# State products of eight running sequences: two products of 64 rows with eight masked blocks, or two of 32 rows with four

## The chip, the cores and the metric

The kernel runs on one core of a Trainium2 chip. The metric is the device time of one execution in microseconds (us). Three executions of the kernel before took 2974.32, 2974.84 and 2976.30 us; the median is 2974.84.

## The reference

The program is one step of a decoder layer: a gated feed-forward block, a mixer, and a second feed-forward block. The mixer has an attention half and a half with a linear recurrence (HGRN2), merged by one output projection. Two request groups share the weights: a prompt of 256 tokens, and 8 running sequences (NB) that each bring 8 new tokens (TS) and a recurrent state. Only the recurrence of the running sequences is touched here. Per sequence b and head h it ends with

```
S = jnp.exp(b_last)[..., None] * S + jnp.einsum(
    'bhsd,bhse->bhde', kc * jnp.exp(b_last[:, :, None] - b), vc)
```

S is a 128 x 128 matrix, kc the decayed keys of the sequence's 8 tokens (8 x 128), vc their values (8 x 128). There are 8 heads and 8 sequences, so 64 such state updates. Everything is float32.

## The kernel before, in words

**Where the work stands.** The recurrence and the first part of the output projection are written out by hand in "beats" (BEATS = 20); each engine has its own loop over the same beats (mix_pe, mix_act, mix_dve), and SyncE issues the loads and stores in mix_sync. Beats 0 to 9 do the four prompt chunks and the scores of the running sequences; beats 10 to 17 do heads 0 to 7 of the running sequences (pe_head, dve_head); beats 12 to 19 the normalisation of each head's output (pe_head_sum, act_head_root, dve_head_scale). The table OUT_AT puts one tile of the output projection (pe_out, 24 products of 128 x 128 by 128 x 320 each, lines L1744 to L1746) into beats 0 to 10, 12, 14, 17, 18 and 19; the tiles 16 to 31 follow after the beats. So head 1 and head 2 stand side by side on TensorE, as do 3 and 4, and 5, 6 and 7, and there is a tile of the projection between the groups.

**One head on TensorE (pe_head).** First the head's outputs: one product of the masked scores with the values (L1902), then for each of the 8 sequences a product of its old state with the decayed queries, 8 columns each (L1904). Then the state products (L1913): the 64 new tokens of all 8 sequences lie on 64 partitions, kst holds the keys (64 x 128 for a head). The values have been copied 8 times into vm, copy b multiplied by a column of gsel that is one on the rows of sequence b and zero elsewhere. A product of kst (64 rows) with four such copies (64 x 512) gives the updates of four sequences in one PSUM bank. There are two: sequences 0 to 3 to bank 6, 4 to 7 to bank 7. A float32 product runs as two passes in the records, each with its own weight load, so the two products are four matrix instructions (32 for the eight heads).

**ScalarE (act_head_values, L1939)** makes the masked copies: 8 activations of 64 x 128 per head, with double buffering over heads. Those of heads 0 and 1 are in beat 9, behind a Silu over all output gates (L2014); those of head h are in beat h + 9.

**VectorE (dve_head)** copies the head's outputs out of PSUM (L1923), multiplies the old states of all 8 sequences by their decay (L1924, 128 x 1024), waits for the state products (semaphore h_sd) and adds bank 6 and bank 7 to the states (L1928, two of 128 x 512). In later beats it normalises the outputs (dve_head_scale: a reciprocal, L1963, and two products, L1966 and L1968), splits them into high and low parts (L1712), and does the evictions and splits of the projection (L1733, L1725).

**What waits for what.** The state products of head h wait for vm of head h (h_vm), and for the adds of head h - 1 (h_sn), which have to empty banks 6 and 7. The copies of head h + 2 wait for the products of head h. Tile 16 of the projection is the first that needs the normalised heads (x_lo), the last of which VectorE makes in beat 20. The old states of heads 4 to 7 are loaded into the buffers of heads 0 to 3 once those have been stored (state_out, state_in).

Of the kernel before, what the change touches and what calls it, by code (L numbers as in the profile page):

```python
# [20 lines left out]
P = 128  # L21
D = 2048
KT = D // P
TP, NB, TS = 256, 8, 8
# [62 lines left out]
def build(nc, io, scr):  # L87
    ctx = ExitStack()
    with ctx:
# [3 lines left out]
        def at(name, off, shape, dt=F32):  # L93
            n = 4
            for d in shape[1:]:
                n *= d
            assert off * KB + n <= 207.8 * KB, (name, off, n)
            return nc.alloc_sbuf_tensor_at(name, shape, dt, offset=BASE + -(-int(off * KB) // 32) * 32)

        s = Sems(lambda n: ctx.enter_context(nc.semaphore(n)))  # L100
        bank = [ctx.enter_context(nc.psum_tensor(f"bank{i}", [P, 512], F32)) for i in range(8)]
# [21 lines left out]
        table = at("table", 3.09375, [33, HEADS])  # L123
        ptab = at("ptab", 3.1875, [1, NB * NPG], I32)
        mask_s = at("mask_s", 3.5, [64, 64])
        gsel = at("gsel", 3.75, [64, NB])
        caus = at("caus", 3.8125, [64, 64])
        kcs = at("kcs", 4.125, [P, 2, NB * 64])
        vcs = at("vcs", 8.125, [64, NB, G * HD])
# [104 lines left out]
        ort = at("ort", 72.625, [P, T])  # L234
        vt = at("vt", 92.125, [P, 3, HG * P])
        kst = at("kst", 104.125, [P, HG * P])
        vm_ = at("vm", 140.125, [64, 2, NB, P])
        dq_ = at("dq", 180.125, [P, 2, HG, 64])
        qi_ = at("qi", 184.125, [P, 2, HG, 64])
        osq_h = at("osq_h", 188.125, [P, 2, T])  # L240
# [835 lines left out]
        def wait_state(eng, h):  # L1076
            eng.wait_ge(s[f"s0_ld{h % SLOTS}"], 16 * (h // SLOTS + 1))
# [812 lines left out]
        def head_bank(h):  # L1890
            return bank[(5, 2)[h % 2]][:, 0:NB * TS]

        def pe_head(pe, h):
            wait_state(pe, h)
            if h == 0:
                pe.wait_ge(s["h_o"], 4)
                pe.wait_ge(s["h_am"], 17)
                pe.wait_ge(s["h_kst"], 10)
            if h >= 2:
                pe.wait_ge(s["h_oe"], h - 1)  # L1900
            o = head_bank(h)
            pe.matmul(o, vt[0:64, 2, h * P:(h + 1) * P], am[0:64, h, :], start=True, stop=False, skip_group_check=True)  # L1902
            for b in range(NB):
                mm = pe.matmul(o[:, TS * b:TS * b + TS], s0[h % SLOTS][:, b, :], qi_[:, 0, h, TS * b:TS * b + TS],  # L1904
                               start=False, stop=b == NB - 1, skip_group_check=True)
            mm.then_inc(s["h_so"], 1)
            pe.wait_ge(s["h_vm"], h + 1)
            if h:
                pe.wait_ge(s["h_sn"], 2 * h)
            else:  # L1910
                pe.wait_ge(s["h_st"], 4)
            for k in range(2):
                mm = pe.matmul(bank[6 + k][:, :], kst[0:64, h * P:(h + 1) * P],  # L1913
                               vm_[:, h % 2, 4 * k:4 * k + 4, :].rearrange("p b e -> p (b e)"), start=True, stop=True)
            mm.then_inc(s["h_sd"], 1)

        def dve_head(dve, link, h):
# [13 lines left out]
        def act_head_values(act, h):  # L1931
            if h == 0:
                act.wait_ge(s["h_sub"], 5 * NC + 2)
                act.wait_ge(s["hv_evd"], 3)
                act.wait_ge(s["h_ebc"], NC + 1)
            if h >= 2:
                act.wait_ge(s["h_sd"], h - 1)
            for b in range(NB):
                ins = act.activation(vm_[:, h % 2, b, :], vt[0:64, 2, h * P:(h + 1) * P], ACT.Copy, scale=gsel[:, b:b + 1])  # L1939
            ins.then_inc(s["h_vm"], 1)  # L1940

# [29 lines left out]
        def mix_pe(pe):  # L1971
            pe_in(pe)
            pe.wait_ge(s["ev"], EV_IN)
            pe.wait_ge(s["s_o"], 4 * NB + 1)
            pe_att_sums(pe)
            pe.wait_ge(s["hv_eva"], 3)
            pe.wait_ge(s["hv_evd"], 3)
            for b in range(BEATS):
                if b < 2 * (NC + 1):
                    if b % 2 == 0:  # L1980
                        pe_hgrn_scores(pe, b // 2)
                    elif b // 2 < NC:
                        pe_hgrn_results(pe, b // 2)
                elif b - 10 < HG:
                    pe_head(pe, b - 10)
                if b >= 12:
                    pe_head_sum(pe, b - 12)
                if b in OUT_AT:
                    pe_out(pe, OUT_AT[b])
            for i in range(KT, N_OUT):  # L1990
                pe_out(pe, i)

        def mix_act(act):
# [9 lines left out]
            for b in range(BEATS + 1):  # L2003
                if b in OUT_AT:
                    act_out(act, OUT_AT[b] + 1)
                if b < 2 * (NC + 1):
                    if b % 2 == 0:
                        if b // 2 < NC:
                            act_decays(act, b // 2 + 1)
                        act_keys(act, b // 2)  # L2010
                    elif b // 2 < NC:
                        act_carried(act, b // 2 + 1)
                    else:
                        act.activation(flat(proj[:, T_HG:T_HG + HG, :]), flat(proj[:, T_HG:T_HG + HG, :]), ACT.Silu)  # L2014
                        act_head_values(act, 0)
                        act_head_values(act, 1)
                if 0 <= b - 9 < HG and b >= 11:
                    act_head_values(act, b - 9)
                if 0 <= b - 11 < HG:
                    act_head_square(act, b - 11)  # L2020
                if 0 <= b - 12 < HG:
                    act_head_root(act, b - 12)
                if 0 <= b - 13 < HG:
                    act_mixed_hi(act, 8 + b - 13)
# [201 lines left out]
def _constants():  # L2226

    import math

    def bucket(dist):  # L2230
        n = np.maximum(dist, 0)
        logn = np.log(np.maximum(n, 1).astype(np.float32) / np.float32(16))
        large = 16 + (logn / np.float32(math.log(64)) * np.float32(16)).astype(np.int32)
        return np.where(n < 16, n, np.minimum(large, 31))

    full = np.arange(LF) - 127
    win = np.arange(LW) - 7
    cs = (PAST + np.arange(TS)[:, None] - (16 * np.arange(64)[None] + 31)).ravel()
    cp = (np.arange(TP)[:, None] - (16 * np.arange(16)[None] + 31)).ravel()
    dist = np.concatenate([full, win, cs, cp])  # L2240
    seen = np.concatenate([full >= 0, (win >= 0) & (win < 512),
                           np.tile(np.arange(64) < 63, TS), (cp >= 0) & np.tile(np.arange(16) < 15, TP)])
    onehot = np.zeros((33, C_ALL), np.float32)
    onehot[np.where(seen, bucket(dist), 32), np.arange(C_ALL)] = 1.0
    r = np.arange(P)
    same = ((r[:, None] // 32 == r[None] // 32) & (r[:, None] % TS == r[None] % TS)).astype(np.float32)
    pair = (r[:, None] // 64 == r[None] // 64).astype(np.float32)
    c = np.arange(64)
    causal = (c[:, None] <= c[None]).astype(np.float32)
    mask = causal * (c[:, None] // TS == c[None] // TS)  # L2250
    seq = (c[:, None] // TS == np.arange(NB)[None]).astype(np.float32)
    cst, bst = 16 * np.arange(64)[:, None], 64 * np.arange(17)[None]
    ov = np.clip(np.minimum(cst + 32, bst + 64) - np.maximum(cst, bst), 0, None) / 32
    ov[63] = 0
    return {"c_ident": np.eye(P, dtype=np.float32), "c_same": same, "c_pair": pair, "c_mask": mask.astype(np.float32),
            "c_seq": seq, "c_causal": causal, "c_overlap": ov.astype(np.float32), "c_onehot": onehot}
# [62 lines left out]
```

## Time and profile before

| | |
|---|---|
| median of three executions | 2974.84 us |
| the profiled execution: its own time | 2973.01 us |
| its span (first to last instruction) | 2971.2 us |
| mean granted TensorE clock | 0.979 of full |
| TensorE products busy | 2911.9 us, 98% of the span |
| VectorE busy | 1474.5 us, 50% |
| ScalarE busy | 988.1 us, 33% |
| the 32 state product instructions (L1913) | 22.0 us busy |

The profiled execution took 1.8 us more than its span, which is what lies before its first and behind its last instruction. Positions such as 1890.05 are us from the start of the span. The heads 0 to 7 of the running sequences lie between 1886 and 1951, the tiles 13 to 17 of the projection between 1951 and 1974. A share of busy time over the whole span says little on so short a stage, so the stage is read by itself: by its chain of waits, by the timeline of each engine, and by the granted clock. That clock has two levels here, 2.4 GHz (1.00 in the rows) and 1.2 GHz (0.50); a value between is a stretch that holds both.

### The profile page before, as it was taken

To read this page: it belongs to the slowest core of one execution; us is meant where nothing else is said; L and a number is where in the kernel's file an instruction comes from. 1 tells how busy PE (TensorE), PEld (TensorE's weight loads), DVE (VectorE), ACT (ScalarE), POOL (GpSimd) and SP (SyncE) were. 2 spreads that over 40 slices of the span, in tenths; PEclk is the share of its full clock that TensorE was granted. 3 is DMA by queue.
4 is the path that set the end of the run, shared out by engine and by line. 5 is a ranking of instruction groups with operands and counts; after the bars stand their busy time and mean duration, and the time that the engine had idled before them with its cause. 6 is when DMAs were issued, how large, how long until landed. Compare 5 with 4: busy or idle time off the path is not lost.

```text
span 2971.2 us, 46821 instructions
## 1 busy us (share of the span) xinstructions
PE 2911.9 (98%) x18952; PEld 2760.5 (93%) x18952; DVE 1474.5 (50%) x1844; ACT 988.1 (33%) x1161; POOL 98.5 (3%) x169
## 2 busy tenths in 40 slices
PE   8999999999999999999999999999999999999999
PEld 5778999999999999998888888789999999999999
DVE  3424444434445444456666667585445434444433
ACT  3433232222323233333332243444433223323222
POOL 2110000000000010110000000010000000000000
PEclk9999999999999999999999997799999999999999
DMA  7364555455545454542336642335545455555354
GB/s 214 100 197 122 146 155 155 127 146 170 151 145 152 121 165 153 195 152 108 103 112 204 207 164 80 111 124 166 152 144 152 122 147 171 149 148 155 116 150 139
DMA packets 637321, 437.46 MB, mean 147 GB/s; under 512 B 20109, under 2 KB 621901, under 8 KB 629661
## 3 DMA queue, kind: packets, MB, share of 16 engines
q1 hardware_dynamic: 634210, 419.13, 46.6%
q0 software_dynamic: 2608, 13.71, 1.5%
q10 hardware_dynamic: 380, 2.93, 0.3%
q8 instruction: 83, 1.36, 0.2%
q14 instruction: 40, 0.33, 0.0%
HBM read 422.33 MB, written 21.65 MB: 149 GB/s over the span
## 4 chain that ended last, share of the span: by engine, by line
PE 95%; DVE 3%; ACT 1%; issue 1%; DMA 0%; ACTq 0%; DVEq 0%
PE bank L410 21%; PE bank L412 21%; PE bank L411 21%; PE bank L748 4%; PE bank L750 4%; PE bank L749 4%; PE bank L673 2%; PE bank L675 2%; PE bank L674 2%; PE bank L1368 2%; PE bank L1744 1%; PE bank L1745 1%; PE bank L1746 1%; PE bank L1197 1%; PE bank L1913 1%
## 5 line engine op out<-in xcount | busy, mean ns | idle before, releaser
L410 PE MATMUL bank<-xh,whi 128*128 128x320 f32 x2816 | 871.5, 309 | 1.3 <-DVE wlo L324 1.3
L411 PE MATMUL bank<-xl,whi 128*128 128x320 f32 x2816 | 871.1, 309 | 0.0
L412 PE MATMUL bank<-xh,wlo 128*128 128x320 f32 x2816 | 871.1, 309 | 0.0
L324 DVE TENSOR_TENSOR wlo<-wraw,whi 128x2048 fp32r<-128x2048 f32 (+1 forms) x305 | 612.6, 2008 | 490.0 <-ACT whi L320 489.1
L320 ACT ACTIVATE whi<-wraw 128x2048 fp32r<-128x2048 f32 (+1 forms) x305 | 513.2, 1683 | 721.5 <-PE bank L412 721.4
L410 PEld LDWEIGHTS bank<-xh,whi 128*128 128x128 f32 x2816 | 529.6, 188 | 2.0 <-issue 1.9
L411 PEld LDWEIGHTS bank<-xl,whi 128*128 128x128 f32 x2816 | 529.7, 188 | 0.0
L412 PEld LDWEIGHTS bank<-xh,wlo 128*128 128x128 f32 x2816 | 529.5, 188 | 0.0
L410 PE MATMUL bank<-hh,whi 128*128 128x320 f32 x1408 | 438.3, 311 | 9.1 <-DVE hl L378 9.1
L411 PE MATMUL bank<-hl,whi 128*128 128x320 f32 x1408 | 437.8, 311 | 0.0
L412 PE MATMUL bank<-hh,wlo 128*128 128x320 f32 x1408 | 437.6, 311 | 0.0
L410 PEld LDWEIGHTS bank<-hh,whi 128*128 128x128 f32 x1408 | 266.7, 189 | 10.2 <-DVE hl L378 10.2
L748 PE MATMUL bank<-xh,whi 128*128 128x320 f32 (+1 forms) x848 | 272.6, 322 | 2.4 <-DVE wlo L733 1.3
L412 PEld LDWEIGHTS bank<-hh,wlo 128*128 128x128 f32 x1408 | 266.8, 189 | 0.0
L411 PEld LDWEIGHTS bank<-hl,whi 128*128 128x128 f32 x1408 | 266.8, 189 | 0.0
L750 PE MATMUL bank<-xh,wlo 128*128 128x320 f32 (+1 forms) x848 | 264.2, 312 | 0.0
L749 PE MATMUL bank<-xl,whi 128*128 128x320 f32 (+1 forms) x848 | 264.0, 311 | 0.0
L340 ACT ACTIVATE sg<-tg 128x320 f32<-128x320 f32 x88 | 41.6, 472 | 448.2 <-DVE tg L362 448.1
L748 PEld LDWEIGHTS bank<-xh,whi 128*128 128x128 f32 (+1 forms) x848 | 160.3, 189 | 27.1 <-issue 24.1
L728 ACT ACTIVATE whi<-wraw 128x2048 fp32r<-128x2048 f32 x52 | 99.4, 1912 | 251.5 <-PE bank L750 245.3
L362 DVE TENSOR_TENSOR tg<-bank,rs 128x320 f32<-128x320 f32 x88 | 43.3, 492 | 243.5 <-PE bank L412 243.5
L749 PEld LDWEIGHTS bank<-xl,whi 128*128 128x128 f32 (+1 forms) x848 | 160.4, 189 | 0.7
(338 smaller groups left out, 3014.0 us busy)
## 6 DMA issues: line engine op xcount, KB each, us to landing
wraw<-in_w_ffn_gate_up SPq DMA_DIRECT2D x176, 1024.0 KB, 5.4
wraw<-in_w_ffn_down SPq DMA_DIRECT2D x128, 704.0 KB, 4.5
wraw<-in_w_mix SPq DMA_DIRECT2D x52, 1024.0 KB, 4.9
pages<-in_cache_cmp SPq DMA_DIRECT2D x128, 128.0 KB, 2.0
oraw<-in_w_mix_out SPq DMA_DIRECT2D x32, 512.0 KB, 3.3
k_sel<-in_slc_k SPq DMA_DIRECT2D x64, 128.0 KB, 2.0
s_v<-in_slc_v SPq DMA_DIRECT2D x64, 128.0 KB
o_win_sample<-in_state_win_kv POOLq DMA_DIRECT2D x8, 1008.0 KB, 15.4
```

Of the source, the lines that this page charges most:

```text
L320: act.activation(whi[:, a % 2, 0:size], wraw[:, a % RAW, 0:size], ACT.Copy).then_inc(s["hi_ready"], 1)
L324: dve.tensor_tensor(wlo[:, a % 2, 0:size], wraw[:, a % RAW, 0:size], whi[:, a % 2, 0:size].bitcast(F32), ALU.subtract).then_inc(s["lo_read ...
L410: pe.matmul(b, whi[:, a % 2, c], h[:, kk, :], start=first, stop=False)
L411: pe.matmul(b, whi[:, a % 2, c], lo_[:, kk, :], start=False, stop=False)
L412: mm = pe.matmul(b, wlo[:, a % 2, c], h[:, kk, :], start=False, stop=end)
L673: pe.matmul(bank[b0 + et][:, :], w1h[:, j, r, e], hi, start=(j, r) == (0, 0), stop=False)
L674: pe.matmul(bank[b0 + et][:, :], w1h[:, j, r, e], lo, start=False, stop=False)
L675: mm = pe.matmul(bank[b0 + et][:, :], w1l[:, j, r, e], hi, start=False, stop=(j, r) == (7, 1))
L728: act.activation(whi[:, g % 2, 0:size], wraw[:, a % 2, 0:size], ACT.Copy).then_inc(s["hi_ready"], 1)
L748: pe.matmul(o, whi[:, g % 2, c], xh[:, k, :], start=k == 0, stop=False)
L749: pe.matmul(o, whi[:, g % 2, c], xl[:, k, :], start=False, stop=False)
L750: mm = pe.matmul(o, wlo[:, g % 2, c], xh[:, k, :], start=False, stop=k == KT - 1)
```

## The change

The 64 rows are split instead of the 8 sequences' copies. Rows 0 to 31 hold sequences 0 to 3, rows 32 to 63 sequences 4 to 7. So the mask gsel gets 4 columns in place of 8, column c being one on the rows of sequence c and of sequence c + 4; vm holds 4 masked copies in place of 8, and each serves both halves. Product k takes rows 32k to 32k + 31 of kst and of vm, 512 columns as before, and writes bank 6 + k as before. Each engine's order is otherwise the same.

```
-        gsel = at("gsel", 3.75, [64, NB])
+        gsel = at("gsel", 3.75, [64, 4])
...
-        vm_ = at("vm", 140.125, [64, 2, NB, P])
+        vm_ = at("vm", 140.125, [64, 2, 4, P])
...
             for k in range(2):
-                mm = pe.matmul(bank[6 + k][:, :], kst[0:64, h * P:(h + 1) * P],
-                               vm_[:, h % 2, 4 * k:4 * k + 4, :].rearrange("p b e -> p (b e)"), start=True, stop=True)
+                r = slice(32 * k, 32 * k + 32)
+                mm = pe.matmul(bank[6 + k][:, :], kst[r, h * P:(h + 1) * P],
+                               vm_[r, h % 2, :, :].rearrange("p b e -> p (b e)"), start=True, stop=True)
             mm.then_inc(s["h_sd"], 1)
...
-            for b in range(NB):
+            for b in range(4):
                 ins = act.activation(vm_[:, h % 2, b, :], vt[0:64, 2, h * P:(h + 1) * P], ACT.Copy, scale=gsel[:, b:b + 1])
...
-    seq = (c[:, None] // TS == np.arange(NB)[None]).astype(np.float32)
+    seq = (c[:, None] // TS % 4 == np.arange(4)[None]).astype(np.float32)
```

In the program the product of 64 rows is placed on a tile of 64 x 128 of the array at row 0; the two of 32 rows are placed on tiles of 32 x 128, the first at row 0, the second at row 32.

ScalarE at the turn from beat 9 to beat 12, before: Silu over the gates, the copies of heads 0 and 1, a split of projection weights (ohi), the copies of heads 2 and 3.

```order
465 L2014 ACT_TABLE_LOAD
466 L2014 ACTIVATE proj<-proj 128x2560
467 L1939 ACTIVATE vm<-vt,gsel 64x128 x16
468 L1721 ACTIVATE ohi<-oraw 128x1024
469 L1939 ACTIVATE vm<-vt,gsel 64x128 x8
470 L1946 ACTIVATE osq_h<-proj 128x320
471 L1721 ACTIVATE ohi<-oraw 128x1024
472 L1939 ACTIVATE vm<-vt,gsel 64x128 x8
```

The same place with the change (lines are one higher).

```order
465 L2015 ACT_TABLE_LOAD
466 L2015 ACTIVATE proj<-proj 128x2560
467 L1940 ACTIVATE vm<-vt,gsel 64x128 x8
468 L1721 ACTIVATE ohi<-oraw 128x1024
469 L1940 ACTIVATE vm<-vt,gsel 64x128 x4
470 L1947 ACTIVATE osq_h<-proj 128x320
471 L1721 ACTIVATE ohi<-oraw 128x1024
472 L1940 ACTIVATE vm<-vt,gsel 64x128 x4
```

Nothing moved: each group of copies has half as many, 32 fewer over the eight heads. On TensorE, VectorE, GpSimd and SyncE the number and the order of instructions are the same; on TensorE only the rows of the state products and their place in the array differ.

## Rows read from the trace of the kernel before

**Rows 1.** The page: span, TensorE, and the chain that ended last, by engine.
```profile
span 2971.2 us, 46821 instructions
PE 2911.9 (98%) x18952; PEld 2760.5 (93%) x18952; DVE 1474.5 (50%) x1844; ACT 988.1 (33%) x1161; POOL 98.5 (3%) x169
...
PE 95%; DVE 3%; ACT 1%; issue 1%; DMA 0%; ACTq 0%; DVEq 0%
```

**Rows 2.** Chain of waits, 1880 to 1960: start us, us, what. State products, heads 0 to 7.
```profile
1890.05 3.68 PE bank L1913 x4
...
1901.20 1.91 PE bank L1913 x4
...
1906.25 3.71 PE bank L1913 x4
...
1918.38 1.91 PE bank L1913 x4
...
1923.27 2.64 PE bank L1913 x4
...
1934.84 1.91 PE bank L1913 x4
...
1939.73 2.04 PE bank L1913 x4
...
1947.26 3.71 PE bank L1913 x4
```

**Rows 3.** Groups by line, 1880 to 1972: count, busy us, mean ns, idle before, releaser.
```profile
L1913 PE MATMUL bank<-vm,kst 64*128 64x512 f32 x32 | 22.0, 821 | 1.4 <-ACT vm L1939 1.4
...
L1939 ACT ACTIVATE vm<-vt,gsel 64x128 f32<-64x128 f32 x64 | 19.4, 387 | 3.5 <-PE bank L1913 3.5
```

**Rows 4.** Timeline of TensorE and of ScalarE at head 0: start us, us, [idle before].
```profile
1886.67 1.95 PE L1904 MATMUL bank<-qi,s 128*128 128x8 f32 x16
1890.05 3.68 PE L1913 MATMUL bank<-vm,kst 64*128 64x512 f32 x4 [1.43 <-ACT vm L1939]
...
1887.58 4.76 ACT L1939 ACTIVATE vm<-vt,gsel 64x128 f32<-64x128 f32 x16
```

**Rows 5.** Timeline of TensorE where products use one column tile, or two.
```profile
1565.52 3.62 PE L1197 MATMUL bank<-pt,vp 128*64 128x512 f32 x8 [1.07 <-issue]
...
1575.80 0.32 PE L1333 MATMUL bank<-same_gt,pcn 128*64 128x128 f32 x1
1575.81 0.64 PE L1315 MATMUL bank<-k_sel,qb 128*64 128x512 f32 x1
```

**Rows 6.** Line L1315, 1543.8 to 1545.2: ns min/median/max, first and last start us.
```profile
L1315 PE MATMUL bank<-k_win,qb x4: 592/592/592, 1544.0 to 1544.5; 128*64 128x512 f32 x4
```

**Rows 7.** Windows, VectorE alone: us, busy (count), granted clock, DMA share, GB/s.
```profile
1886.00:1921.60 35.60, 16.84 (x23) 0.76 0.38 119
1921.60:1970.60 49.00, 43.59 (x57) 0.79 0.38 118
```

**Rows 8.** Timeline of VectorE, first and last of six waits in that second stretch.
```profile
1934.94 0.23 DVE L1923 COPY proj<-bank 128x64 f32<-128x64 f32 x1 [1.95 <-PE bank L1904]
...
1958.31 1.23 DVE L1725 TENSOR_TENSOR olo<-oraw,ohi 128x1024 fp32r<-128x1024 f32 x1 [0.67 <-ACT ohi L1721]
```

**Rows 9.** Timeline of TensorE at tiles 16 and 17 of the projection.
```profile
1968.28 0.41 PE L1744 MATMUL bank<-xh,ohi 128*128 128x320 f32 x1 [0.41 <-DVE xl L1712]
...
1970.59 0.42 PE L1744 MATMUL bank<-xh,ohi 128*128 128x320 f32 x1 [0.98 <-DVE olo L1725]
```

**Rows 10.** Chain of waits: projection products at either clock.
```profile
1896.70 0.27 PE bank L1745
...
1897.34 0.15 PE bank L1745
```

**Rows 11.** Windows of all engines: us; PE, PEld, DVE, ACT, POOL busy; granted clock; DMA.
```profile
1903.11:1909.96 6.85, 6.85 (x24) 4.22 (x22) 4.18 (x6) 4.09 (x10) 0.00 (x0) 0.55 0.69 213
...
1916.14:1921.03 4.89, 4.89 (x25) 3.12 (x25) 1.99 (x4) 0.00 (x0) 0.00 (x0) 1.00 0.00 0
...
1893.70:1954.00 60.30, 60.30 (x247) 44.24 (x247) 44.59 (x59) 25.94 (x70) 0.00 (x0) 0.73 0.44 135
```

**Rows 12.** SyncE and TensorE: first reload of a state, landing time (us), its reader.
```profile
1904.97 0.58 SPq L1073 DMA_DIRECT2D s<-in_state_hgrn  x1
...
s<-in_state_hgrn SPq DMA_DIRECT2D x4, 512.0 KB, 4.4
...
1921.32 1.95 PE L1904 MATMUL bank<-qi,s 128*128 128x8 f32 x16
```

## The prediction, as put on record before the run

> **What bounds the kernel now.** I read the page first. TensorE is busy for 98% of the span and holds 95% of the chain that ended last [rows 1]: what shortens TensorE's row shortens the kernel, unless another engine is close behind at that place. So I then read the stage of the change, by the chain of waits between 1880 and 1960. All eight groups of state products stand on it, 3.68, 1.91, 3.71, 1.91, 2.64, 1.91, 2.04 and 3.71 us, together 21.5 us [rows 2]; that nearly matches the 22.0 us of the whole line [rows 3]. The same four instructions take 1.91 us in one head and 3.71 in another. The windows say why: the granted clock is 1.00 around head 3 and 0.55 around head 2 [rows 11]. That is 2.4 and 1.2 GHz, and before each fall the engine had been in the short products of L1904 or waiting. Third, the timelines of the engines that TensorE could come to wait for. ScalarE's copies hold it up once, before head 0, for 1.43 us [rows 4]; the line has no other wait on ScalarE [rows 3]. VectorE has much room in the first half, busy 16.8 us of 35.6, but from 1921.6 to 1970.6 it is busy 43.6 us of 49.0, and TensorE waits for it at the end of that stretch, 0.41 and 0.98 us [rows 7, 9]. So there are two near-bounds in the second half, TensorE and VectorE.
>
> **ScalarE: half of the copies go.** The 16 copies of heads 0 and 1 take 4.76 us, 0.30 us each from start to start [rows 4]. Head 0's own eight end at about 1887.6 + 2.4 = 1890.0, and the state products start at 1890.05. With four they end 1.2 us earlier, at 1888.8. TensorE is through with L1904 at 1886.67 + 1.95 = 1888.6, so 1.2 of its 1.43 us of waiting go, and 0.2 stay. In the other heads ScalarE is early already, so the other 28 removed copies (8.4 us of ScalarE) are worth nothing by themselves; they let the split of projection weights behind the copies of heads 0 and 1 start 2.4 us sooner, which VectorE was waiting for. Term 1: -1.2 us.
>
> **TensorE: the same columns, other rows.** Each product still streams 512 columns in two passes, so one product by itself costs what it did; halving its rows saves nothing. Serially the group stays at 1.91 us (at 2.4 GHz), four passes at 0.43 us plus 0.2. What is new is that the two products lie on different rows of the array, read different partitions, and write different banks. Whether the hardware then runs them side by side the trace of before cannot show for rows, since no two neighbours in it use different row tiles. It shows it for columns. L1315 puts two products on column tiles 0 and 64. The four passes start between 1544.0 and 1544.5 [rows 6]; one after the other at 0.43 us the fourth would start 1.3 us behind the first. And a pass of L1315 starts 0.01 us after one of L1333 on the other tile, with other weights and another bank [rows 5]. Where all products are on one column tile (L1197), eight passes take 3.62 us, no overlap [rows 5]. So the bounds for the group are 1.91 us (nothing overlaps; a little more, if the narrower tile costs a switch) and 2 x 0.43 + 0.1 = 0.96 us (all overlaps). I take the second, as the nearest row is of the same data type and the same 512 columns. Over the eight groups that halves 21.5 us: -10.4 us, with 0.05 us a group kept for the start-up. Term 2, as far as TensorE alone decides.
>
> The Trainium skill bears on this in two ways (TensorE: Matmul & The Clock Gate, Part 3, the section on packing small matmuls). It says that products on different groups of 32 rows run concurrently, 3.07 times as fast for four of them; by that the group is 0.96 us, as by the column rows. But it also says that matmuls start and end strictly in program order. Taken literally, with the order pass 1, pass 2, pass 1, pass 2, only the middle two could overlap. The trace's pairs of starts on L1315 [rows 6] do not agree with that; no run here shows it for rows. It is the second rival below.
>
> **What VectorE lets through.** Heads 0 to 3: half of 3.68 + 1.91 + 3.71 + 1.91 is 5.6 us, with term 1 6.8 us. VectorE idles 18.8 us in that stretch [rows 7], so all of it counts. Heads 4 to 7: half of 2.64 + 1.91 + 2.04 + 3.71 is 5.15 us, and the two waits at tiles 16 and 17 would add 1.4. But VectorE has only six waits there, from 1.95 to 0.35 us, 4.7 us together (the first and the last of them are [rows 8]). The stretch cannot shrink by more. The state products of head h wait for VectorE's adds of head h - 1; in heads 6 and 7, TensorE will arrive first and wait there, since VectorE has a reciprocal of 2.2 us and three more instructions between two heads. I take 4.2 of the 4.7: a hand-over or two stays exposed. Then TensorE waits longer before tile 16 than the 0.41 us of now, for some 3 to 5 us, and the clock may be at 1.2 GHz after it; ten projection products at 0.27 in place of 0.15 us [rows 10] cost 1.2. I take +1.0. For the clock within the heads I assume the share it has now.
>
> Loads: the first reload of a state is issued at 1904.97, right behind the adds of head 1, and lands in 4.4 us; head 4 reads it at 1921.3 [rows 12]. The adds come some 4 us sooner and head 4 about 9, so 7 us of cover remain. This cover is gone only if a load takes over 11 us.
>
> **Sum.** -6.8 - 4.2 + 1.0 = -10.0 us. Against the profiled execution that is 2973.0 - 10.0 = 2963.0 us (its span plus 1.8 around it). That execution lies 1.8 us under the median of the runs shown, 2974.84, so the forecast for the median is 2964.8 us.
>
> **Rivals.**
> 1. *No overlap on row tiles.* Then only term 1 is left: 2974.8 - 1.2 = 2973.6 us. For it: both products feed all 128 output columns, where the column tiles of [rows 5, 6] share nothing on the output side. Against it: each writes its own bank, which is what a row tile needs.
> 2. *Only the middle passes overlap*, three steps in place of four. Heads 0 to 3 give 11.2 / 4 + 1.2 = 4.0 us; heads 4 to 7 2.6 and most of the 1.4 us of waits that VectorE's lag makes, less what the cold restart costs, about 2.5. Together 6.5: 2968.3 us. For it: program order. Against it: [rows 6].
> 3. *The clock takes it back: slower.* While the state products run overlapped, and while TensorE waits for VectorE, the engine has less to do, and in every row so far the level fell after such stretches. Between 1893.7 and 1954, 60.3 us, the mean clock is 0.73 [rows 11], so 46% of it, 27 us, is at 2.4 GHz. If all that ran at 1.2 GHz, it would take 1.87 times as long (3.71 against 1.91, 0.27 against 0.15): +23.7 us. All state products are then the slow ones, 29.7 us, of which the overlap takes 14.8, and terms 1 and the waits take 2.6: net +6.3, 2981 us. It turns from gain to loss once about 15 of the 27 us are lost (12.8 us of TensorE gain over 0.87 us lost for each). Against it: VectorE bounds the second half, so part of a slower TensorE is hidden there, and in heads 1, 3 and 5 the level held through a group at 2.4 GHz.
>
> The other way, the clock could rise: at 0.76 over the first stretch [rows 7] some 17 of 35.6 us are at 1.2 GHz, and at 2.4 GHz they would be 8 us shorter, with VectorE free to follow. Half of such a gain, 2961 us, is as far as I reckon with.
>
> **How the numbers follow.** Full overlap with VectorE behind it: 0.68, 2964.8 us, its own range 2960 to 2969. No overlap: 0.15. Middle passes only: 0.10. The clock: 0.07. The range of 8 in 10 reaches down to 2960, for a clock that rises, and up to the first rival, 2974.2; only the clock case and tails stay outside. A difference under 0.2% (5.9 us, so down to 2968.9) counts as no change here. Faster than that: nearly all of the forecast and half of rival 2, 0.71. Within: rival 1, the other half of rival 2, tails, 0.22. Slower: 0.07.
>
> **What would show it.** In the changed kernel's profile the group of L1914 should be about 0.96 us at 2.4 GHz and 1.9 at 1.2, with its four passes starting in two pairs; three steps of 0.43 mean rival 2, four rival 1. The wait on vm before head 0 should be 0.2 us or gone. VectorE should run almost without a wait from head 4 to tile 16, TensorE should show new waits for the adds (L1928) in heads 6 and 7 and a longer one for xl at tile 16. I am wrong if the group takes 1.9 us at full clock, or if the granted clock over 1886 to 1960 falls well below the 0.77 or so of now.

## The result, and the profile after

The changed kernel takes 2965.46 us (median of 10 runs, 2960.99 to 2972.09) against 2974.82 us (10 runs, 2971.95 to 2979.2) of the kernel before: 9.4 us less, ratio 0.997, 95% interval 0.9962 to 0.9978 (6.5 to 11.3 us less). The forecast was 2964.8. The profiled execution took 2964.03 us, its span is 2962.2.

The page of the changed kernel: span, TensorE and ScalarE, the chain by engine. It answers to [rows 1].

```profile
span 2962.2 us, 46789 instructions
...
PE 2905.2 (98%) x18952; PEld 2757.5 (93%) x18952; DVE 1474.0 (50%) x1844; ACT 978.7 (33%) x1129; POOL 98.6 (3%) x169
...
PE 95%; DVE 3%; ACT 1%; issue 1%; DMA 0%; ACTq 0%; DVEq 0%
```

There are 32 instructions fewer on ScalarE and none fewer on TensorE, and the kernel is bound by TensorE as before. The chain of waits of the changed kernel, 1880 to 1960 (start us, us, what), answers to [rows 2]. All eight groups of state products are shown, with the products of L1904 of heads 1, 2, 4, 5 and 6.

```profile
1884.55 1.87 PE bank L1914 x4
...
1892.86 1.88 PE bank L1904 x16
1894.74 1.68 PE bank L1914 x4
...
1897.04 3.51 PE bank L1904 x16
1900.55 2.01 PE bank L1914 x4
...
1910.35 1.06 PE bank L1914 x4
...
1912.76 3.51 PE bank L1904 x16
1916.27 2.01 PE bank L1914 x4
...
1924.80 1.88 PE bank L1904 x16
1926.68 1.06 PE bank L1914 x4
...
1928.84 3.16 PE bank L1904 x16
1932.00 2.01 PE bank L1914 x4
...
1939.50 2.01 PE bank L1914 x4
```

A group at 2.4 GHz (heads 3 and 5) is 1.06 us, where it was 1.91; at 1.2 GHz (heads 2, 4, 6 and 7) it is 2.01, where it was 3.71. The groups of heads 0 and 1 (1.87 and 1.68) lie across a change of level. Together the eight are 13.7 us, 7.8 less. The other thing to see is L1904: in heads 4 to 6 it was 1.88 us each time in the kernel before and is now 3.51, 1.88 and 3.16; over heads 1 to 7, where it stands on the chain, it rose from 15.9 to 19.3 us, with the same instructions. That is the clock. How much of it is chance is taken up below.

How the passes lie, in the group of head 3 of the changed kernel (the view of line L1914 from 1910 to 1912; ns min/median/max, first and last start us). It answers to [rows 6].

```profile
L1914 PE MATMUL bank<-vm,kst x4: 587/640/692, 1910.3 to 1910.8; 32*128 32x512 f32 x4
```

The four records start at 1910.284, 1910.291, 1910.818 and 1910.824: two 7 ns apart, two 6 ns apart, and 0.53 us between the pairs. The records do not name the product that a pass belongs to. I read the first pair as both first passes and the second as both second passes, because two passes on one row tile start at least 0.43 us apart in every kernel here. At 1.2 GHz (head 2) it is the same picture with 1.01 us between the pairs.

Timeline of TensorE in the changed kernel at head 0 and at tiles 16 and 17, to compare with [rows 4] and [rows 9].

```profile
1882.33 1.95 PE L1904 MATMUL bank<-qi,s 128*128 128x8 f32 x16
1884.55 1.87 PE L1914 MATMUL bank<-vm,kst 32*128 32x512 f32 x4 [0.27 <-ACT vm L1940]
...
1959.12 0.41 PE L1744 MATMUL bank<-xh,ohi 128*128 128x320 f32 x1 [0.41 <-DVE xl L1712]
1961.44 0.42 PE L1744 MATMUL bank<-xh,ohi 128*128 128x320 f32 x1 [0.98 <-DVE olo L1725]
```

The wait for vm fell from 1.43 to 0.27 us. At the tiles the same two waits stand, to the hundredth, 9.2 us earlier. The timeline shows no other wait of TensorE in the stage: none for the adds of L1929.

Timeline of VectorE in the changed kernel from 1917 to 1966, its five waits. It answers to [rows 8], where there were six in the 49 us.

```profile
1926.79 0.23 DVE L1924 COPY proj<-bank 128x64 f32<-128x64 f32 x1 [2.38 <-PE bank L1904]
...
1935.97 2.15 DVE L1964 RECIPROCAL ors_h<-ort_h 128x320 f32<-128x320 f32 x1 [0.34 <-ACT ort_h L1959]
...
1948.00 0.49 DVE L1733 TENSOR_TENSOR xt<-xt,bank 128x320 f32<-128x320 f32 x1 [0.67 <-PE bank L1746]
1949.15 1.23 DVE L1725 TENSOR_TENSOR olo<-oraw,ohi 128x1024 fp32r<-128x1024 f32 x1 [0.66 <-ACT ohi L1721]
...
1965.26 0.49 DVE L1733 TENSOR_TENSOR xt<-xt,bank 128x320 f32<-128x320 f32 x1 [2.34 <-PE bank L1746]
```

VectorE still waits 4.05 us for others before tile 16 (the first four), so it did not become the bound in heads 4 to 7. From its wait at 1949.15 on, the chain is VectorE's own work up to tile 16, as before: 9.97 us in either kernel (1949.15 to 1959.12, and 1958.31 to 1968.28). That is why the two waits at the tiles are the same.

Windows of 70 us from head 0 on, the first of the kernel before, the second of the changed kernel (us, busy of PE, PEld, DVE, ACT, POOL, granted clock, DMA).

```profile
1886.31:1956.31 70.00, 68.57 (x281) 49.81 (x281) 47.70 (x63) 32.91 (x88) 0.00 (x0) 0.73 0.41 128
```

```profile
1881.97:1951.97 70.00, 69.73 (x312) 54.73 (x312) 51.23 (x66) 25.76 (x60) 0.00 (x0) 0.68 0.42 129
```

More work fits in the same 70 us (312 products against 281) at a lower clock.

**How far two profiles can be compared.** Head 0 already starts 4.3 us earlier in the changed kernel (1881.97 against 1886.31), where both run the same instructions up to that point. The clock falls and rises at other places in the two executions, and the traces drift apart and together in steps of about 1.5 us; between two profiles of the kernel before, further down, the lead goes from 1.3 to 2.8 to 4.3 us ahead of head 0. Only 4.8 us of the 9.0 us between the two spans arise between head 0 and tile 16. So the single pair shows what a group costs, but not what the kernel gained; for that I use medians, and the stage's length in several profiles.

### The profile page after: what moved, and what is told of

It reads as the page before. It is cut to its first block, busy times and chain, and to the rows that moved or that the text cites. A ratio compares the mean times of both kernels' runs of the same rounds, so it can differ in the third digit from the quotient of the medians.

```text
span 2962.2 us, 46789 instructions
## 1 busy us (share of the span) xinstructions
PE 2905.2 (98%) x18952; PEld 2757.5 (93%) x18952; DVE 1474.0 (50%) x1844; ACT 978.7 (33%) x1129; POOL 98.6 (3%) x169
## 4 chain that ended last, share of the span: by engine, by line
PE 95%; DVE 3%; ACT 1%; issue 1%; DMA 0%; ACTq 0%; DVEq 0%
PE bank L410 21%; PE bank L411 21%; PE bank L412 21%; PE bank L748 4%; PE bank L750 4%; PE bank L749 4%; PE bank L673 2%; PE bank L675 2%; PE bank L674 2%; PE bank L1368 2%; PE bank L1744 1%; PE bank L1745 1%; PE bank L1746 1%; PE bank L1197 1%; PE bank L2201 1%
## 5 line engine op out<-in xcount | busy, mean ns | idle before, releaser
L728 ACT ACTIVATE whi<-wraw 128x2048 fp32r<-128x2048 f32 x52 | 99.4, 1912 | 251.5 <-PE bank L750 245.2
## 6 DMA issues: line engine op xcount, KB each, us to landing
pages<-in_cache_cmp SPq DMA_DIRECT2D x128, 128.0 KB, 2.1
k_sel<-in_slc_k SPq DMA_DIRECT2D x64, 128.0 KB, 2.0
s_v<-in_slc_v SPq DMA_DIRECT2D x64, 128.0 KB
```

Of the source, the lines that this page charges most:

```text
L728: act.activation(whi[:, g % 2, 0:size], wraw[:, a % 2, 0:size], ACT.Copy).then_inc(s["hi_ready"], 1)
```

## Experiments

The table gives, for the kernels that keep the order of the tiles and VectorE's work, the sum of the eight groups on the chain of the profiled execution, and the median time (number of runs). "Stage" is the time from the start of head 0 to the start of the last product of the projection, read from each trace. Comparisons are each against runs of the kernel before on the same chip, whose medians were 2974.2 to 2975.0.

| kernel | groups, us | stage, us | median us (runs) | ratio, 95% interval |
|---|---|---|---|---|
| before | 21.5 | 137.1 | 2974.8 (10) | |
| before once more | 24.6 | 143.0 | 2974.2 (11) | 0.9991 to 1.0009 |
| changed | 13.7 | 132.2 | 2965.5 (10) | 0.9962 to 0.9978 |
| same tile for both | 24.2 | 142.5 | 2977.0 (11) | 1.0001 to 1.0019 |
| eight copies | 13.9 | 133.4 | 2964.0 (5) | 0.9950 to 0.9977 |
| four copies, 64 rows | 22.5 | 139.0 | 2972.7 (11) | 0.9985 to 1.0003 |
| products one by one | 27.4 | 146.2 | 2981.0 (11) | 1.0016 to 1.0034 |
| changed, products twice | 24.5 | 142.5 | 2970.9 (11) | 0.9981 to 0.9999 |
| the same, second time | 21.6 | 136.1 | 2970.8 (11) | 0.9979 to 0.9997 |
| before, products twice | 49.3 | 167.1 | 3003.8 (4) | 1.0078 to 1.0109 |

**Both products on one row tile.** The rivals were: the gain is overlap of row tiles; or the copies.

```
-                r = slice(32 * k, 32 * k + 32)
+                r = slice(0, 32)
```

> Both products of a head take rows 0 to 31 of keys and values (so the updates of sequences 4 to 7 are left out, those of 0 to 3 made twice); count, columns, banks and copies as in the changed kernel. Theory (the gain is the overlap of two row tiles): the four passes start one after the other, the group takes 1.91 us at 2.4 GHz and 3.7 at 1.2, and only the shorter wait for the copies is left, about 2973.5 us. Rival (32 rows are faster than 64 by themselves, or four copies are): group near 1.0 us, about 2965.5 us.

Measured: 2976.95 us, ratio 1.001 (1.0001 to 1.0019). The view of line L1914 in this kernel, group of head 1:

```profile
L1914 PE MATMUL bank<-vm,kst x4: 587/587/692, 1898.4 to 1899.8; 32*128 32x512 f32 x4
```

and its chain of waits, heads 0 to 2:

```profile
1887.35 3.67 PE bank L1914 x4
...
1898.48 1.91 PE bank L1914 x4
...
1903.87 3.71 PE bank L1914 x4
```

The same shapes as in the changed kernel, but the passes start over 1.4 us in place of 0.5, and the group is back at 1.91 and 3.71. Both products still write their own bank. So 32 rows are as dear as 64, and what a group saves is the overlap of two different row tiles (which also means rows of different partitions; no run parts the two). The Trainium skill says the same of a single product (TensorE: Matmul & The Clock Gate, Why this matters for your kernels): one of 32 rows takes as long as one of 128. The whole gain is lost. I had expected 2973.5, a little under the kernel before, for the shorter copies; that is not seen here.

**Eight copies with the new products.** vm holds eight blocks again, of which the products read the first four, made last.

```
-        vm_ = at("vm", 140.125, [64, 2, 4, P])
+        vm_ = at("vm", 140.125, [64, 2, 8, P])
...
-                               vm_[r, h % 2, :, :].rearrange("p b e -> p (b e)"), start=True, stop=True)
+                               vm_[r, h % 2, 0:4, :].rearrange("p b e -> p (b e)"), start=True, stop=True)
...
-            for b in range(4):
-                ins = act.activation(vm_[:, h % 2, b, :], ..., ACT.Copy, scale=gsel[:, b:b + 1])
+            for b in (4, 5, 6, 7, 0, 1, 2, 3):
+                ins = act.activation(vm_[:, h % 2, b, :], ..., ACT.Copy, scale=gsel[:, b % 4:b % 4 + 1])
```

> The changed kernel with the copies as costly as before: each head makes four copies that nothing reads and then the four that are read. Theory: the overlap stays, group 1.06 us at 2.4 GHz, the wait before head 0 is 1.4 to 2.6 us again, in the other heads nothing waits for ScalarE; about 1.2 us over the changed kernel, 2966.7 us. Rival (the copies carry the gain, as ScalarE's share of the stage): back to 2973 to 2975 us.

Measured: 2963.98 us (5 runs), ratio 0.9964 (0.9950 to 0.9977), no different from the changed kernel. The timeline of TensorE in it has its one wait of the stage:

```profile
1889.54 1.97 PE L1914 MATMUL bank<-vm,kst 32*128 32x512 f32 x4 [1.43 <-ACT vm L1940]
```

The wait of 1.43 us is back exactly, and the median is not higher. Term 1 is a real wait that goes, but 1.2 us is below what five or ten runs tell apart.

**Four copies with the old products.** The other half of the change. GpSimd zeroes blocks 4 to 7 of vm once, ahead of head 0.

```
+            if h == 0:
+                pe.wait_ge(s["vm_zero"], 1)
...
-            for b in range(NB):
+            for b in range(4):
...
+            pool.memset(vm_[:, :, 4:8, :], 0.0).then_inc(s["vm_zero"], 1)
```

> The kernel before with four masked copies a head in place of eight (blocks 4 to 7 are zero, so the updates of sequences 4 to 7 are left out); two products of 64 rows. Theory: only the wait of head 0 gets shorter, 1.2 us, about 2973.6 us, no change that can be told. Rival (copies): about 2966 us.

Measured: 2972.72 us (11 runs), ratio 0.9994 (0.9985 to 1.0003): 1.5 us less than before, but an interval that holds none at all. Groups at 1.91 and 3.71. By that interval the copies alone bring at most 4.5 us; the trace shows the 1.2 us of the wait at head 0.

**The kernel before, once more,** for a second profile of it.

> The kernel before, unchanged, as a second profile of it. Theory (in the first pair of profiles 4.3 of 9.0 us had been gained before head 0, where both kernels are alike, which is the clock's chance): the same 2975 us, ratio 1.000, with the start of head 0 some us off 1886.3 and the stretch from head 0 to tile 17 within 2 us of 84.3 us. Rival (the change moves something before head 0): head 0 at 1886.3 within 0.5 us.

Measured: 2974.22 us, ratio 1.000 (0.9991 to 1.0009). Its chain of waits, heads 0, 1 and 3:

```profile
1885.43 3.78 PE bank L1913 x4
...
1897.55 3.38 PE bank L1913 x4
...
1916.41 1.91 PE bank L1913 x4
```

Its groups sum to 24.6 us where those of [rows 2] sum to 21.5, its stage is 143.0 us against 137.1, and yet the spans are within 1 us, since head 0 starts at 1881.69. So the 4.3 us by which the changed kernel's profile is ahead at head 0 are no more than the kernel before differs from itself. And two profiles of one kernel differ by 6 us in the stage: more than I had expected of it.

**Each second product waits for the first.** Is it really the overlap, with nothing else different?

```
             for k in range(2):
...
+                if k:
+                    mm.then_inc(s["h_first"], 1)
+                    pe.wait_ge(s["h_first"], h + 1)
```

(The wait stands between the two products; the product in front raises the semaphore.)

> The changed kernel where the second product waits for a semaphore that the first raises at its end; two row tiles, four copies, nothing left out. Theory: no overlap, group about 2.1 us at 2.4 GHz and 4.0 at 1.2 with the hand-over, 2976 to 2978 us, like the kernel with both products on one row tile. Rival (the placement on narrower tiles gains by itself): under 2972 us.

Measured: 2980.98 us, ratio 1.0025 (1.0016 to 1.0034). Chain of waits of this kernel in head 1:

```profile
1896.11 1.06 PE bank L1917 x2
1897.17 0.04 issue
1897.21 1.12 PE bank L1917 x2
```

One product alone takes 1.06 us, what two take side by side; two in a row with the hand-over take 2.22, more than the 1.91 of back-to-back ones. A group of four passes is four times 0.43 and 0.2 of start-up; here the 0.2 stands twice (1.06 and 1.12). I had expected 2976 to 2978: I had counted the hand-overs too low. Groups +13.7 us against the changed kernel, median +15.5.

**The products twice, in both kernels.** The write is the same one again, so this prices a group as the kernel sees it.

```
-            for k in range(2):
+            for k in (0, 1, 0, 1):
```

> The changed kernel with each head's two state products made twice over, the same values to the same banks (8 more groups). Theory (a group costs what its row says, 1.06 us at 2.4 GHz and 2.01 at 1.2): with the clock shares of now 8 x 1.6 = 13 us more than the changed kernel, less what hides behind VectorE: 2976 to 2979 us. Rival (the overlap only shows in the records, the array does the same work in the same time): 21 us more, 2987 us.

> The kernel before with each head's two state products made twice over. Theory: 8 groups at 1.91 or 3.71 us, 8 x 2.8 = 22 us over the kernel before, 2996 us, so 18 us over the doubled changed kernel, twice the gain of the change. Rival (the gain is not in these products): as far from the doubled changed kernel as the single ones are from each other, 9 us.

Measured: 2970.85 us for the changed kernel with it (+5.4), 3003.84 for the kernel before with it (+29.7). So twice as many products of the new kind are no dearer than one set of the old (ratio to the kernel before 0.9981 to 0.9999), and less dear than the 13 us that I had expected; twice as many of the old cost 29.7 us, where I had expected 22. The profile of the first did not fit its median: it was of an execution of 2979.6 us, with groups of 24.5 us. So it was run once more.

> The same kernel as the doubled one before it: the changed kernel with its two state products issued twice a head, on 32 rows each. Its first comparison gave 2970.9 us, 5.4 above the changed kernel, while its profiled execution, one of 2979.6, had groups that sum to 24.5 us, 10.7 above those of the changed kernel (13.8). If the groups' sum is what counts, the comparison comes out near 2976, and a second profile shows groups of 1.92 us at 2.4 GHz and 3.71 at 1.2 with about the same total. If most of the doubled work ran beside something or the clock paid for part of it, the median stays at 2969 to 2972 and the groups are fewer at 3.71: each group that is at 2.4 GHz in place of 1.2 is worth 1.8 us, so three more of them explain the 5.3 us.

Measured: 2970.79 us, the same again. Chain of waits of that second profile, heads 0 to 6 without 4:

```profile
1887.14 3.56 PE bank L1914 x8
...
1898.27 1.92 PE bank L1914 x8
...
1903.56 3.71 PE bank L1914 x8
...
1915.66 1.92 PE bank L1914 x8
...
1932.13 1.92 PE bank L1914 x8
...
1937.03 2.12 PE bank L1914 x8
```

Eight passes take 1.92 or 3.71 us, as four old ones do. The groups sum to 21.6 us here and to 24.5 in the first profile, with two groups at 3.71 against four; the difference is the clock's, in one and the same kernel. The median of the first comparison is nearer to this lower sum, but its +5.4 stays under the +7.9 of the groups. I leave the 2.5 us open: they are within the two intervals.

**VectorE with less to do.** Is VectorE the bound in heads 4 to 7, as the prediction has it? The eight reciprocals of the norm (2.15 us each) become copies.

```
-            dve.reciprocal(ors_h[:, h % 2, :], ort_h[:, h % 2, :]).then_inc(s["o_rs"], 1)
+            dve.tensor_copy(ors_h[:, h % 2, :], ort_h[:, h % 2, :]).then_inc(s["o_rs"], 1)
```

> The changed kernel with the eight reciprocals of the head normalisation replaced by copies of the same tile (so the normalisation is left out), which takes 1.8 us of VectorE from each of eight beats, 14 us in all. Theory of the prediction (VectorE sets the second half of the heads): 3 to 5 us faster than the changed kernel, 2961 us. Rival (TensorE sets it all through, since its clock is lower there): only the waits before tiles 16 and 17 go, 1.4 us, 2964 us, and a few hand-overs.

Measured: 2961.38 us (5 runs), ratio 0.9953 (0.9939 to 0.9967), 4.1 us under the changed kernel. VectorE's windows in the second half: of the changed kernel, and behind it of this one.

```profile
1917.60:1961.40 43.80, 39.01 (x51) 0.75 0.36 109
```

```profile
1917.60:1961.40 43.80, 27.80 (x49) 0.74 0.39 121
```

The chain of waits in this kernel, state products of heads 4 to 6:

```profile
1911.03 1.06 PE bank L1914 x4
...
1916.77 2.01 PE bank L1914 x4
...
1927.34 1.06 PE bank L1914 x4
```

Eleven us of VectorE's work are gone from that window, and from the start of head 4 to that of head 7 it takes 23.03 us (1912.75 to 1935.78), against 23.22 (1912.08 to 1935.30) in the changed kernel. So from head 4 to head 7 VectorE bounds nothing. What goes are the two waits at tiles 16 and 17, 1.4 us; the stage is 2.1 us shorter. The median says 4.1; for the rest no row speaks, and the two intervals touch. The expectation from the VectorE theory was hit in its number by luck: the rows refute it.

**Where the last projection tiles stand.** If more useful work lay between the heads, would the clock stay up? Three orders; the changed kernel has tiles 11 to 15 at beats 12, 14, 17, 18 and 19.

```
+        OUT_AT = {**{b: b for b in range(11)}, 12: 11, 14: 12, 16: 13, 18: 14, 19: 15}
...
+        OUT_AT = {**{b: b for b in range(11)}, 11: 11, 13: 12, 15: 13, 17: 14, 19: 15}
...
+        OUT_AT = {**{b: b for b in range(11)}, 11: 11, 12: 12, 14: 13, 16: 14, 18: 15}
```

> The changed kernel with the projection tiles 11 to 15 in beats 12, 14, 16, 18, 19 in place of 12, 14, 17, 18, 19: no three heads in a row, tile 13 between heads 6 and 7. Theory (three heads in a row keep the clock at 1.2 GHz and the tile after them pays): 1 to 3 us faster, 2963 us. Rival (VectorE has more to do between heads 6 and 7 then and holds the state products): same or 1 us slower.

> The changed kernel with tiles 11 to 15 in beats 11, 13, 15, 17, 19. The orders of heads and tiles is then 1 T 2 3 T 4 5 T 6 7 T T. Theory (the clock): two heads in a row at most, 1 to 3 us faster, 2963 us. Rival (a tile between two heads only moves the same work): no change, 2965.5 us.

> The changed kernel with tiles 11 to 15 in beats 11, 12, 14, 16, 18: one tile each after heads 1, 2, 4 and 6, and only one behind head 7. Theory (the clock): heads 1 and 2 and what follows at 2.4 GHz; but behind head 7 TensorE has less to do while VectorE finishes the normalisation, so it waits some us before tile 16: 2964 to 2968 us. Rival (VectorE has room): 2962 us.

Measured: 2965.31, 2963.97 and 2965.48 us (8, 5 and 8 runs), ratios 0.9969, 0.9964 and 0.9971: none can be told from the changed kernel. For the first order the window of 70 us from head 0, and for the third TensorE's waits at the tiles:

```profile
1884.40:1954.40 70.00, 68.40 (x352) 55.28 (x352) 56.58 (x73) 27.68 (x63) 0.00 (x0) 0.80 0.46 141
```

```profile
1952.56 0.41 PE L1744 MATMUL bank<-xh,ohi 128*128 128x320 f32 x1 [1.55 <-DVE olo L1725]
...
1956.13 0.42 PE L1744 MATMUL bank<-xh,ohi 128*128 128x320 f32 x1 [1.11 <-DVE xl L1712]
...
1959.71 0.63 PE L1744 MATMUL bank<-xh,ohi 128*128 128x320 f32 x1 [2.87 <-DVE xl L1712]
...
1962.02 0.63 PE L1744 MATMUL bank<-xh,ohi 128*128 128x320 f32 x1 [0.34 <-DVE olo L1725]
```

The clock over such a window was 0.80, 0.68 and 0.78 in the three orders, against 0.68 in the changed kernel; in the first, 352 products stand in it in place of 312. The waits at the tiles were 3.0, 3.5 and 5.9 us, against 1.4. So TensorE runs further ahead of VectorE and gives part of it back. But these orders also leave fewer tiles between head 7 and the first that needs the heads, so they do not show that a higher clock alone brings the waits. The first order's stage is 128.0 us, 4.2 under the changed kernel's, with the same median: again the pair of profiles says more than the medians bear out. No version beats the changed kernel by what can be told.

## Why the prediction was right, and where it was not

**The overlap (term 2): right.** The passes start in two pairs, not in three steps and not in four, so rivals 1 and 2 are out for the group. The forecast of 0.96 us was 1.06: the group is one product by itself, 1.06 with its start-up (shown by the products one by one), where I had 0.86 + 0.1. At 1.2 GHz 2.01 against 1.9. With these, the groups of [rows 2] become some 12 us in place of 21.5; 13.7 were measured, at a worse mix of levels. The Trainium skill's rule that matmuls start and end strictly in program order (TensorE: Matmul & The Clock Gate, Part 3) does not agree with this trace if each pass counts as a matmul: by the reading of the pairs above, the second product's first pass starts 7 ns behind the first's, ahead of the first's second pass. For whole products the trace agrees: they start 7 ns apart and end 6 ns apart, in order. Rival 2 had taken the rule pass by pass. The Trainium skill's rule on packing rows, in the same part, agrees, at a factor of 1.8 for two tiles (1.91 to 1.06).

**Term 1, the copies: right in the trace, 1.43 to 0.27 us.** In the median it can't be seen: with the wait put back it was 1.5 us lower, with four copies alone 1.5 lower than before.

**The failed step is VectorE's cap in heads 4 to 7**, with its sequel, "in heads 6 and 7, TensorE will arrive first and wait there", and the +1.0 for a cold start behind a longer wait before tile 16. The prediction capped the second half at 4.2 us, took 1.0 off again, and held the clock within the heads fixed, so L1904 stayed at 1.88 us in heads 4 to 6. It was 3.51, 1.88 and 3.16. From head 4 to tile 16 the changed kernel took 47.0 us (1912.08 to 1959.12), the one before 47.3 (1920.96 to 1968.28): the groups saved 3.2 us (10.3 to 7.1), L1904 took back 2.9. So TensorE stayed the bound, VectorE kept 4.05 us of waits, and the waits at the tiles did not grow. Lighter VectorE work left heads 4 to 6 as long as they were, which shows that VectorE did not hold them. Whether the cap would bind at a higher clock is not shown: where the waits at the tiles grew, the tiles had been moved too.

**This pair is a poor measure of the second half, though.** From head 4 to tile 16 the six profiles with groups at 1.91 and 3.71 took 47.3 to 53.8 us, 50.4 on average; that of the kernel before is the shortest of them. The changed kernel and the one with eight copies took 47.0 each, 3.4 less, close to the 3.2 that the prediction had left for it. In heads 0 to 3 it is the other way: 6.8 us were forecast, the pair gives 4.5 (34.65 to 30.11), and the averages 3.8 (34.5 to 30.7). In the pair 4.6 us of groups and 1.2 of waiting went there, and a lower level in L1904 and around it took back 1.2. So the clock, held fixed in the sum, was missing in both halves.

**The clock (rival 3): not taken back as priced, but perhaps in part.** Rival 3 (+6.3 us) is refuted by the 9.4 us gained. A lower clock was named as a sign of being wrong, and over the same work, head 0 to tile 16, it did fall, from 0.77 to 0.71 (over 1886 to 1960, the stretch that the prediction named, the kernel before had 0.75). But the kernel before had 0.71 in its second profile, and the six with slow groups 0.71 to 0.77; over 70 us they had 0.66 to 0.73, the changed kernel 0.68. So the share by itself tells nothing. L1904 says more. On the chain of heads 1 to 7 it took 15.9 to 19.1 us in the six, 17.2 on average, and 19.3, 19.4 and 19.2 in the changed kernel, with eight copies and with lighter VectorE work; all three ran it at 3.51 us in head 4, which only two of the six did. That fits some 2 us that the clock takes back. If so, it goes with the short groups and not with the overlap, since the two profiles with the new products twice, which overlap as well, had 17.3 and 15.9. With three profiles against six, the nearest of them 0.1 us apart, it is not shown, and chance is not shown either. The reason that I gave against this rival, that VectorE hides part of it, is not what the rows show.

**The sum.** -10.0 was forecast, -9.4 measured (-6.5 to -11.3). By the stage's length, six profiles with groups at 1.91 and 3.71 (before twice, same tile, four copies, twice twice) average 140.0 us, and the two with overlapped single groups (changed, eight copies) 132.8: -7.2. The groups alone are 9.3 less in them (23.1 to 13.8), and L1904 2.1 more. By the profiles of before and after alone it was -4.9. From 13.7 to 49.3 us of groups the median goes from 2965.5 to 3003.8: 38.4 us for 35.6, so about what a group costs reaches the end. The overlap was forecast rightly, and it carries the gain. That the whole came within 0.7 us of the forecast was partly luck: a cap that did not bind and a restart that did not come had taken 3.3 us off the sum (6.55 to 3.2), and the clock that I had held fixed took back about as much in the pair (2.9).

**What stays open.** Kernels whose groups take about the same time, with four copies each, had medians of 2977.0, 2972.7 and 2970.8 us (same tile, four copies with 64 rows, changed with products twice), where one price of 2973.5 was expected. They lie up to 6 us apart, more than their intervals explain, and no run here shows the cause. So a few us of the 9.4 could be something other than the groups. Two products on different row tiles with the same bank were not run.

## What to carry to other kernels

Two float32 products of 32 rows and 512 columns on different row tiles, with different banks, took the time of one (1.06 us); so when a contraction of 64 rows has a block structure, split the rows, and don't expect anything from fewer rows on one tile. If TensorE's clock moves between two levels in a stage, take prices of single groups from a profile, but the gain from medians of ten runs: two profiles of one kernel differed by 6 us in the stage. The same holds for shares of the gain: a half of the stage that seems to have saved nothing may only stand against a lucky profile of the kernel before. Before you cap a gain by another engine, count the path at both levels: here a cap worked out at the clock of one trace did not bind.

## What the runs showed of the hardware that I had not expected

- Passes of two products on two row tiles start in pairs 6 to 7 ns apart, and do not wait for each other's second pass. With twice the products the pairs go on without a gap: in the second profile of that kernel they start at 1898.20, 1898.74, 1899.17 and 1899.60, 0.43 us apart after the first.
- The granted clock over 70 us from head 0 on was 0.66 to 0.73 in two profiles of the same kernel, and the stage 137.1 or 143.0 us. With the tiles of the projection moved it was 0.80, 0.68 and 0.78 in three orders.
- In the kernel before with its products twice, five of the eight groups take 7.1 to 7.2 us, so they ran at 1.2 GHz for the whole of eight long passes.
- A hand-over by a semaphore from TensorE to itself shows as 0.04 us of issue, but costs 0.3 us a group at 2.4 GHz with the start-up paid twice (1.06 + 0.04 + 1.12 against 1.91).
